# Second chunk pair's backward inverses moved from tile to tile by the sync engine

## The chip, the cores and the metric

The kernel runs on one core of one Trainium2 chip. The metric is the device time of one execution in microseconds (us). The engines are called by the names of the profile: PE is TensorE, DVE is VectorE, ACT is ScalarE, POOL is GpSimd and SP is the sync engine, which here only waits on semaphores and issues transfers.

## What is computed

One layer of a hybrid encoder on 1024 tokens of width 1024, in float32. The part that matters here is group A, a bidirectional RWKV-7 time mixing with 8 heads of 64, whose recurrence per token and direction is

```python
Sa = einsum('zbhij,zbhj->zbhi', S, at)
S  = S * wt[..., None, :] + Sa[..., :, None] * bt[..., None, :] + vt[..., :, None] * kt[..., None, :]
y  = einsum('zbhij,zbhj->zbhi', S, rt)
```

Group B is a windowed attention (128 keys to each side, distance penalty, a sink logit). Both group outputs go through one output projection and a residual, then a gated feed-forward with a width-3 convolution, and a last RMSNorm.

## The kernel before

The recurrence is done in chunks of 32 tokens (`C = 32`, `NC = 32` chunks). Within a chunk the delta rule is a triangular system, so for each chunk and head a 32x32 inverse is built beforehand. `TI[z]` holds those inverses for direction z (0 forward, 1 backward), with 4 head pairs times 32 chunks on the 128 partitions and the 32x32 matrix of one head of the pair along the free axis (`e` is the head of the pair). VectorE fills `TI[0]` and then `TI[1]` by forward substitution, two operations per row (lines 1969 and 1973), and counts rows in `sol_row`. GpSimd then stores them to DRAM as `TI_d` (line 1664 for z = 0, line 1678 for z = 1, eight transfers each, one per head pair and head), from where the scan loads them in another layout: in `TIs[slot]` the 32 rows of an inverse lie on 32 partitions.

The scan (`chunk_steps` on TensorE) takes one forward and one backward chunk per step, two steps per slot, two slots, so four steps per iteration i, and eight iterations. Slot 0 and slot 1 have each a set of tiles (`AGB`, `UV`, `TIs`, `Ys`). One step is: products with the loaded values (line 924), with the state (line 937), attention scores or probabilities in between (lines 875, 885), the product with the inverse (line 960), then state (975) and output (984). A slot's first step waits for `scan_full[slot]`, which counts all loads of that slot's tiles, 16 for each transfer. The attention scores of a slot's first step wait for `qk_full`, the loads of `q_d` and `kk_d` (line 489).

The forward inverses of the first two chunk pairs are loaded from `TI_d` early. For the backward direction the first chunks needed are the last ones, and `TI[1]` is complete only when the scan could start. So for slot 0 the kernel does not go through DRAM: SP (head 0, line 520) and ACT (head 1, line 1320) copy, for each of 2 chunks and 4 head pairs, one partition of `TI[1]` onto 32 partitions of `TIs[0]`, 4 KB each. Each of them then adds one to `moves_issued`. GpSimd waits for 2 of it, then issues the eight stores of `TI[1]`, and then waits for the first filling of slot 1 (`scan_full[1]`), after which it reloads the last five of the eight 512 KB tiles of x (`x_load`, line 1670). SP, after its eight copies, waits for all eight stores (`TI1_stored`), loads slot 1's backward inverses from `TI_d` (`load_inverses(1, 1)`, line 502, two transfers of 32 KB), and enters its loop. There it waits for step 2's products, issues `load_scan` of slot 0's next tiles (lines 474, 479, 482: ten transfers, 1.9 MB), four stores of y (532), and then `load_qk` for the next attention block (489).

`Ys[1]` lies where `TI[1]` lay, and `xT` where the first layer's operands lay, which is why ACT waits before its third output copy (line 1392) and GpSimd before `x_load`.

## Time and profile before

| | us |
|---|---|
| three runs | 1379.25, 1374.97, 1375.43 |
| their median | 1375.43 |
| the profiled execution's own time | 1381.39 |
| span of its profile | 1379.4 |
| mean granted TensorE clock | 0.962 |

The 2.0 us between the profiled time and the span lie outside the profiled instructions. Times inside the trace count from the span's start. The place of the change is the start of the scan, near 346 to 390 us of the span.

### The profile page before, as it was taken

Reading aid. Unit: us, or ns where it says so; the run is one execution under the profiler, and the core shown is the slowest. Engines: PE = TensorE matmul, PEld = TensorE weight load, DVE = VectorE, ACT = ScalarE, POOL = GpSimd, SP = SyncE. Lnnn points to the kernel's source line nnn. Section 1 sums busy time; section 2 is a strip of 40 time slices with the busy share of each in tenths; the row PEclk is TensorE's granted clock in tenths of the full one; section 3 lists DMA queues with packets and bytes.
Section 4 is the critical chain, followed back from the end, with each engine's and each line's share of the span. In section 5 each row is a group of like instructions: output and inputs, shape, how many; then the busy total and the mean of one; then the engine's idle time right before and its main releaser. Section 6 shows DMA issues by size and latency. Waiting matters only on the chain.

```text
span 1379.4 us, 28338 instructions
## 1 busy us (share of the span) xinstructions
PE 1281.8 (93%) x11280; PEld 1001.4 (73%) x11280; DVE 857.1 (62%) x1094; ACT 521.9 (38%) x729; POOL 231.2 (17%) x242
## 2 busy tenths in 40 slices
PE   6999999897589988889999999999999999999997
PEld 2476776775356655567778888888888888888886
DVE  4986687799557777783398555565555573333345
ACT  3735345221246656742144333333333342111221
POOL 1001001021312233400005222222222110000000
PEclk9999999999669989999989999999999999999998
DMA  5038758697666776502313222333222455322103
GB/s 212 20 92 188 173 149 200 182 257 181 162 203 214 237 219 208 173 31 98 131 46 92 76 68 85 91 91 87 66 76 91 137 176 208 114 97 72 49 31 123
DMA packets 145830, 179.53 MB, mean 130 GB/s; under 512 B 52432, under 2 KB 107792, under 8 KB 145776
## 3 DMA queue, kind: packets, MB, share of 16 engines
q1 hardware_dynamic: 136384, 152.16, 36.9%
q0 software_dynamic: 4288, 12.98, 3.4%
q10 hardware_dynamic: 5104, 13.67, 3.1%
q8 instruction: 34, 0.56, 0.2%
q14 instruction: 20, 0.16, 0.0%
HBM read 121.16 MB, written 57.54 MB: 130 GB/s over the span
## 4 chain that ended last, share of the span: by engine, by line
PE 75%; DVE 11%; DMA 5%; issue 3%; SPq 3%; ACT 2%; POOL 2%; DVEq 0%; ACTq 0%; POOLq 0%
PE banks L1107 28%; PE banks L695 18%; PE banks L677 6%; PE banks L1144 5%; PE banks L683 3%; DVE work L1969 2%; DVE work L1973 2%; PE banks L1081 2%; PE banks L659 2%; PE banks L885 2%; PE banks L901 1%; DMA work<-y_d 1%; DMA work<-in_w_in 1%; PE banks L1089 1%; PE banks L975 1%
## 5 line engine op out<-in xcount | busy, mean ns | idle before, releaser
L1107 PE MATMUL banks<-op,sw_hi 128*128 128x512 f32 x1120 | 344.8, 389 | 0.0
L1107 PEld LDWEIGHTS banks<-op,sw_hi 128*128 128x128 f32 x1120 | 210.3, 188 | 43.7
L1107 PE MATMUL banks<-op,sw_lo 128*128 128x512 f32 x560 | 217.8, 389 | 0.0
L2162 DVE TENSOR_TENSOR xT<-xT,banks 128x1024 f32<-128x1024 f32 x23 | 28.1, 1221 | 150.4 <-PE banks L695 150.4
L1107 PEld LDWEIGHTS banks<-op,sw_lo 128*128 128x128 f32 x560 | 105.1, 188 | 21.7
L1477 ACT ACTIVATE sw_hi<-work 128x1024 fp32r<-128x1024 f32 (+1 forms) x60 | 72.1, 1203 | 112.2 <-PE banks L1107 110.1
L1765 DVE TENSOR_TENSOR sw_lo<-work,sw_hi 128x1024 fp32r<-128x1024 f32 (+1 forms) x60 | 84.9, 1416 | 37.5 <-ACT sw_hi L1477 37.5
L677 PE MATMUL banks<-ph_hi,pw_hi 128*128 128x512 f32 x272 | 87.7, 404 | 6.4 <-DVE work L1887 3.1
L1739 POOL TENSOR_TENSOR work<-work 128x512 f32<-128x512 f32 x20 | 28.4, 1418 | 387.0 <-DMA work<-in_w_gu 245.9
L677 PE MATMUL banks<-ph_hi,pw_lo 128*128 128x512 f32 x272 | 86.2, 399 | 0.0
L695 PE MATMUL banks<-g_hi,down_hi 128*128 128x512 f32 x256 | 79.0, 390 | 0.0
L695 PE MATMUL banks<-g_hi,down_lo 128*128 128x512 f32 x256 | 78.8, 389 | 0.0
L695 PE MATMUL banks<-g_lo,down_hi 128*128 128x512 f32 x256 | 78.8, 389 | 0.0
L1407 ACT ACTIVATE down_hi<-work 128x1024 fp32r<-128x1024 f32 (+1 forms) x18 | 18.5, 1035 | 134.2 <-PE banks L695 128.8
L677 PEld LDWEIGHTS banks<-ph_hi,pw_hi 128*128 128x128 f32 x272 | 51.3, 193 | 21.6 <-issue 7.8
L683 PE MATMUL banks<-ph_lo,pw_hi 128*128 128x512 f32 x272 | 64.4, 389 | 0.0
L1689 POOL TENSOR_TENSOR work<-work 128x384 f32<-128x384 f32 x60 | 48.2, 834 | 87.1 <-DVE work L2021 87.1
L1522 ACT ACTIVATE hT<-banks,par 128x1024 f32<-128x1024 f32 x20 | 22.4, 1118 | 103.9 <-DVE banks L2252 103.9
L1644 POOL DMA_DIRECT2D work<-scan_d x32 | 20.5, 648 | 241.6 <-DMA scan_d<-work 241.3
L677 PEld LDWEIGHTS banks<-ph_hi,pw_lo 128*128 128x128 f32 x272 | 52.5, 193 | 11.4
L683 PEld LDWEIGHTS banks<-ph_lo,pw_hi 128*128 128x128 f32 x272 | 51.1, 188 | 10.6
L695 PEld LDWEIGHTS banks<-g_hi,down_hi 128*128 128x128 f32 x256 | 47.9, 188 | 10.3 <-DVE g_lo L1765 0.5
(277 smaller groups left out, 2492.4 us busy)
## 6 DMA issues: line engine op xcount, KB each, us to landing
work<-scan_d SPq DMA_DIRECT2D x32, 768.0 KB, 4.8
work<-in_w_gu SPq DMA_DIRECT2D x88, 256.0 KB, 4.6
scan_d<-work SPq DMA_DIRECT2D x16, 1024.0 KB, 5.3
g_d<-hT SPq DMA_DIRECT2D x22, 512.0 KB, 2.9
scan_d<-work SPq DMA_DIRECT2D x32, 256.0 KB, 6.6
work<-in_w_down SPq DMA_DIRECT2D x16, 512.0 KB, 3.6
work<-in_w_in ACTq DMA_DIRECT2D x15, 512.0 KB, 3.7
work<-g_d SPq DMA_DIRECT2D x15, 512.0 KB, 4.4
```

What stands on the lines that cost most here:

```text
L659: mm = pe.matmul(out[:, h * HALF:(h + 1) * HALF], wt[:, k, :], src[:, k, h * HALF:(h + 1) * HALF], start=(k == 0), stop=(k == kn - 1))
L677: pe.matmul(out[:, h * HALF:(h + 1) * HALF], w_[:, k, :], ph_hi[:, k, h * HALF:(h + 1) * HALF], start=(k == 0 and w_ is pw_hi[slot]), stop ...
L683: mm = pe.matmul(out[:, h * HALF:(h + 1) * HALF], pw_hi[slot][:, k, :], ph_lo[:, k, h * HALF:(h + 1) * HALF], start=False, stop=(k == KD - 1))
L695: mm = pe.matmul(out[:, h * HALF:(h + 1) * HALF], wp[slot][:, k, :], xp[k][:, h * HALF:(h + 1) * HALF], start=(opens and k == (ks or range ...
L885: mm = pe.transpose(banks[:, 4 + kb, (2 * e + hh) * P:(2 * e + hh + 1) * P], Pr[g][:, h, kb * P:(kb + 1) * P], ident[:, :])
L1107: mm = pe.matmul(banks[:, 3 * slot + bank, :], w[:, n, k * P:(k + 1) * P], x[n][:, k, :], start=(opens and k == 0 and p_ == 0), stop=(k == ...
L1144: mm = pe.matmul(banks[:, 6 * slot + i % 2, :], w[m][:, k, :], x[g][:, token_half[h]], start=(k == 0 and p_ == 0), stop=(k == fn - 1 and p ...
L1477: act.activation(sw_hi[:, lo_:hi_, :], wsrc[slot][:, lo_:hi_], ACT.Copy).then_inc(fs["w_hi"], 1)
L1689: p = pool.tensor_tensor(Pr[g][:, h, :], Pr[g][:, h, :], rinv[:, h:h + 1].broadcast_to([P, BAND]), ALU.mult)
L1739: pool.tensor_tensor(x[:, 1], x[:, 7], x[:, 6], ALU.add).then_inc(fs["sums"], 1)
L1765: tt(out, x, hi.bitcast(F32), ALU.subtract).then_inc(done, 1)
L2162: tt(x, x, product, ALU.add).then_inc(added[slot], 1)
```

## The change

After its eight copies for slot 0 and its increment of `moves_issued`, SP issues sixteen more copies of the same form, which fill `TIs[1]` from `TI[1]` for both heads of the pair. The two loads from `TI_d` (`load_inverses(1, 1)`) are gone. SP's wait for `TI1_stored` stays, now directly ahead of its loop, since later iterations read `TI_d`. The first filling of slot 1 counts 8 transfers plus 16 in place of 10, which is `SLOT1_FIRST`, and the waits on `scan_full[1]` on TensorE and GpSimd use it. ACT gets one more wait ahead of its third output copy, since that copy writes where `TI[1]` lies.

```diff
@@ -378,6 +378,7 @@
             return n - GROUPS[GROUP_OF[n]][0] + (8 if GROUP_OF[n] == 1 else 0)
 
 
+        SLOT1_FIRST = 8 + 4 * NPAIR
         V_STORES = 16 * 2 * (P // C)
 
 
@@ -519,8 +520,12 @@
                     at = C * j + NC - 2 + cc
                     sp.dma_start(TIs[0][x_rows(0, 1, C), 1, cc, j, :], TI[1][at:at + 1, 0]).then_inc(inverse_moved[1 - cc], 16)
             sp.sem_inc(s["moves_issued"], 1)
+            for cc in (1, 0):
+                for j in range(NPAIR):
+                    at = C * j + NC - 4 + cc
+                    for e in range(2):
+                        sp.dma_start(TIs[1][x_rows(e, 1, C), 1, cc, j, :], TI[1][at:at + 1, e]).then_inc(scan_full[1], 16)
             sp.wait_ge(s["TI1_stored"], 16 * 2 * NPAIR)
-            load_inverses(1, 1)
             y_rows = y_d.rearrange("z (c t) (e n) -> z c e t n", t=C, e=2)
 
             def store_y(i, slot):
@@ -915,7 +920,7 @@
                     if lead and q == 0:
                         pe.wait_ge(scan_full[slot], 16 * 8)
                     elif cc == 0:
-                        pe.wait_ge(scan_full[slot], 16 * 10 * i + 16 * (10 - 2 * (slot == 0)))
+                        pe.wait_ge(scan_full[slot], 16 * 10 * i + 16 * (SLOT1_FIRST if slot else 8))
                     pe.wait_ge(s["S_add"], n + FREE)
                     for j in range(NPAIR):
                         for z, c2 in enumerate(c2s):
@@ -1387,6 +1392,7 @@
                         if first == 0 and q == 2:
                             for moved in inverse_moved:
                                 act.wait_ge(moved, 16 * 2 * NPAIR)
+                            act.wait_ge(scan_full[1], 16 * SLOT1_FIRST)
                             act.wait_ge(s["TI1_stored"], 16 * 2 * NPAIR)
                         act.wait_ge(ys_stored[slot], 64 * i + FREE)
                         act.activation(y_move(slot, cc), banks[:, 2 * cc:2 * cc + 2, 0:256], ACT.Copy).then_inc(s["Y_out"], 1)
@@ -1677,7 +1683,7 @@
                 for e in range(2):
                     pool.dma_start(TI_d[1, e][:, :, j].rearrange("s c t -> c s t"), TI[1][C * j:C * (j + 1), e])\
                         .then_inc(s["TI1_stored"], 16)
-            pool.wait_ge(scan_full[1], 16 * 10)
+            pool.wait_ge(scan_full[1], 16 * SLOT1_FIRST)
             x_load(range(3, KD))
             pool.wait_ge(s["TI_stored"], 16 * 2 * NPAIR)
             pool.wait_ge(s["TI1_stored"], 16 * 2 * NPAIR)
```

SP's queue at this place, between the loads of the forward inverses and the loop (`work<-work` is a copy from `TI[1]` to `TIs`, `TI_d` the inverses in DRAM). Before:

```order
L502 DMA work<-TI_d 32x256 x3
L520 DMA work<-work 32x1x32 [waits sol_row,scan_full0,va_stored]
L520 DMA work<-work 32x1x32 x7
L502 DMA work<-TI_d 32x256 [waits TI1_stored]
L502 DMA work<-TI_d 32x256
L547 UNCONDITIONAL_BRANCH
L474 DMA work<-scan_d 128x1536 [waits S_mm,Y_mm]
L479 DMA work<-TI_d 32x256
L482 DMA work<-v_d 32x2x256
L479 DMA work<-TI_d 32x256
L482 DMA work<-v_d 32x2x256
```

With the change:

```order
L503 DMA work<-TI_d 32x256 x3
L521 DMA work<-work 32x1x32 [waits sol_row,scan_full0,va_stored]
L521 DMA work<-work 32x1x32 x7
L527 DMA work<-work 32x1x32 x16
L552 UNCONDITIONAL_BRANCH [waits TI1_stored]
L475 DMA work<-scan_d 128x1536 [waits S_mm,Y_mm]
L480 DMA work<-TI_d 32x256
L483 DMA work<-v_d 32x2x256
L480 DMA work<-TI_d 32x256
L483 DMA work<-v_d 32x2x256
```

Sixteen copies stand where two loads from `TI_d` stood, and the wait for `TI1_stored` has moved from ahead of those loads to behind the copies, onto the loop's entry; the sequence after it is the same.

GpSimd's queue at the same place. Before:

```order
L1670 DMA xT<-in_xT 128x1024 [waits qkv_mm]
L1670 DMA xT<-in_xT 128x1024 x2
L1678 DMA TI_d<-work 32x32x32 [waits moves_issued,sol_row]
L1678 DMA TI_d<-work 32x32x32 x7
L1670 DMA xT<-in_xT 128x1024 [waits scan_full1]
L1670 DMA xT<-in_xT 128x1024 x4
```

With the change:

```order
L1676 DMA xT<-in_xT 128x1024 [waits qkv_mm]
L1676 DMA xT<-in_xT 128x1024 x2
L1684 DMA TI_d<-work 32x32x32 [waits moves_issued,sol_row]
L1684 DMA TI_d<-work 32x32x32 x7
L1676 DMA xT<-in_xT 128x1024 [waits scan_full1]
L1676 DMA xT<-in_xT 128x1024 x4
```

No row moved: the stores still wait for `moves_issued`, and the five loads of x for `scan_full[1]`, whose count is now reached by copies and not by loads from `TI_d`.

## Rows read from the trace of the kernel before

**Rows 1.** The page: its first line and the shares of the chain by engine.

```profile
span 1379.4 us, 28338 instructions
...
PE 75%; DVE 11%; DMA 5%; issue 3%; SPq 3%; ACT 2%; POOL 2%; DVEq 0%; ACTq 0%; POOLq 0%
```

**Rows 2.** TensorE in order of time: start, length, row, [idle before it <-releaser].

```profile
359.34 0.65 PE L984 MATMUL banks<-work 32*32 32x64 f32 x32
366.37 1.13 PE L924 MATMUL banks<-work 32*64 32x64 f32 x32 [6.38 <-DMA work<-TI_d]
...
386.29 1.65 PE L875 MATMUL banks<-work 64*128 64x384 f32 x4 [2.38 <-DMA work<-kk_d]
```

**Rows 3.** The chain that ended last, 325 to 415 us: start, length, what.

```profile
351.46 0.02 SPq L521
...
357.57 6.63 DMA TI_d<-work
...
365.17 0.36 SPq L474
...
369.23 1.42 SPq L479
...
373.88 12.37 DMA work<-kk_d
```

**Rows 4.** GpSimd's queue in order of time, 340 to 392 us.

```profile
352.08 6.28 POOL L1678 DMA_DIRECT2D TI_d<-work  x8 [16.51 <-SPq L521]
366.62 2.68 POOL L1670 DMA_DIRECT2D xT<-in_xT  x5 [8.27 <-DMA work<-TI_d]
```

**Rows 5.** Stretches: us of each engine, PEclk, DMA share, GB/s.

```profile
core 0: us, PE busy (x) PEld busy (x) DVE busy (x) ACT busy (x) POOL busy (x), PEclk, DMA share, GB/s
360.00:362.00 2.00, 0.00 (x0) 0.00 (x0) 1.37 (x5) 1.29 (x3) 0.00 (x0) 0.72 0.87 117
362.00:364.00 2.00, 0.00 (x0) 0.00 (x0) 0.00 (x0) 0.02 (x1) 0.00 (x0) 0.50 0.07 21
364.00:366.00 2.00, 0.00 (x0) 0.00 (x0) 0.00 (x0) 0.00 (x0) 0.00 (x0) 0.50 0.10 33
366.00:368.00 2.00, 1.63 (x52) 1.51 (x56) 0.00 (x0) 0.00 (x0) 1.38 (x3) 0.50 0.83 264
...
372.00:376.00 4.00, 3.99 (x132) 2.89 (x128) 2.14 (x6) 2.00 (x6) 0.47 (x1) 0.68 1.02 400
...
384.00:388.00 4.00, 1.71 (x11) 0.64 (x15) 0.40 (x2) 0.98 (x3) 0.00 (x0) 0.50 0.97 321
```

**Rows 6.** Line 520, the first pair's moves: issue in ns, and landing.

```profile
L520 SPq DMA_DIRECT2D work<-work x8: 591/608/803, 346.0 to 350.8; - x8
...
DMA to landing us min/median/max: 1.8/1.9/2.2
```

**Rows 7.** Line 502 in 364 to 366 us, the two loads taken out.

```profile
L502 SPq DMA_DIRECT2D work<-TI_d x2: 317/368/418, 364.2 to 364.6; - x2
...
DMA to landing us min/median/max: 1.7/1.7/1.7
```

**Rows 8.** VectorE in order of time, the end of the second step.

```profile
360.31 0.69 DVE L2095 TENSOR_TENSOR work<-work,PC 128x512 f32<-128x512 f32 x1
```

**Rows 9.** DMA queues (packets, MB, share) during the moves, 346 to 352 us.

```profile
q10 hardware_dynamic: 384, 0.03, 4.7%
q1 hardware_dynamic: 336, 0.03, 4.1%
```

**Rows 10.** DMA queues during GpSimd's stores, 351 to 366 us.

```profile
q0 software_dynamic: 384, 1.05, 52.3%
```

**Rows 11.** TensorE in order of time, one stop that no row names.

```profile
409.07 0.36 PE L937 MATMUL banks<-work 64*64 64x64 f32 x1 [2.58 <-issue]
```

**Rows 12.** Line 1244 at 309 us, a load beside GpSimd's earlier stores.

```profile
L1244 ACTq DMA_DIRECT2D work<-in_w_in x1: 334/334/334, 309.4 to 309.4; - x1
...
DMA to landing us min/median/max: 3.5/3.5/3.5
```


## The prediction

> **What bounds the kernel now.** I read the page first. The span is 1379.4 us and three quarters of the chain is PE work [rows 1]; transfers hold 5% of it and SP's issuing 3%, so only a place where the chain leaves PE can give something to a change of transfers. The second view is PE in order of time around the start of the scan. Step 2 ends its output products at 359.34 + 0.65 = 359.99 us, and step 3, the first on slot 1, starts at 366.37 after 6.38 us of idleness that a load from `TI_d` ended. A second stop follows soon: the scores of iteration 1 start at 386.29 after 2.38 us of waiting for `kk_d` [rows 2].
>
> The third view is the chain between the two stops, to see what each waits on [rows 3, 4]. SP signals its moves as issued at 351.46. GpSimd starts its eight stores at 352.08, the last one's issue begins at 357.57, and all have landed 6.63 us later, at 364.20. Then SP issues the two loads of line 502, which landed before PE's 366.37 and before GpSimd starts its five loads of x at 366.62. SP enters its loop and issues the next `load_scan` from 365.17 on. Everything from there to the issue of `kk_d` at 373.88 is SP issuing without a gap, and `kk_d` takes 12.37 us to land. So PE's first stop hangs on the landing of the inverses, but the chain goes past PE: it goes over `TI1_stored`, SP's issuing and the `kk_d` transfer, and PE waits for that once more.
>
> The fourth view is the DMA share in stretches [rows 5]. It is 0.87 while the stores run (360 to 362 us), 0.07 and 0.10 in the next two stretches, 0.83 in 366 to 368, and 1.02 and 0.97 later, up to `kk_d`'s landing. The engines of the DMA are full nearly from 366 to 386 us. That is why a 384 KB load takes 12.37 us there.
>
> **The change, part by part.**
>
> *Sixteen moves more on SP.* The form is that of line 520: 8 issues of 591 to 803 ns, landing after 1.8 to 2.2 us [rows 6]. The eight issues and their gaps fill 346.02 to 351.46 us, 0.68 us each. Sixteen more from 351.48 end at 351.48 + 16 x 0.68 = 362.4; the last starts at 361.7 and lands 1.9 us later, at 363.6. I add 0.3 us for the stores beside them: 363.9. What could make this shorter is that the first eight were issued while ACT issued its own eight; the two loads taken out needed 317 and 418 ns each [rows 7]. At 0.42 + 0.04 us the last move would start at 351.48 + 15 x 0.46 = 358.4 and land near 360.4. What could make it longer is a rival below. I take 0.68 since it is the same form on the same queue.
>
> *PE's first stop.* PE could start step 3 at 361.00 at the earliest, when DVE's scaling of the state ends (360.31 + 0.69) [rows 8]. With the moves landed at 363.9 it starts there and not at 366.37: 2.5 us earlier (bounds: 366.37 - 361.0 = 5.4 us, and nothing). What waits behind it (ACT's and DVE's copies, exponentials) comes forward with it.
>
> *The two loads taken out.* The two issues of line 502 took 0.317 and 0.418 us, with a gap of 0.05 us behind each: 0.84 us of SP's time goes, out of the 0.97 us between the end of its wait (364.20) and the first load of the loop (365.17) [rows 3, 7]. Against it stands that the moves take room from the stores, and SP still waits for the stores. Eight moves of ACT and seven of SP took 4.7% + 4.1% of 6 us, so sixteen take 0.5 us of each DMA engine [rows 9]. The stores keep those engines at 52.3% of 15 us, 7.8 us, and in 352 to 362 us they are nearly full [rows 5, 10]. If all 0.5 us is added, the stores land at 364.7. SP enters its loop 0.84 - 0.5 = 0.3 us earlier; at best 0.84. The moves themselves end at 362.4, before 364.2, so SP's extra issuing (11 us) is hidden under a wait it had anyway. That cover is 1.8 us thick.
>
> *GpSimd.* Its stores are issued as before. Its wait for slot 1's tiles now ends near 363.9 and the five loads of x, 2.5 MB, start 2.5 us earlier, at about 364.1, ahead of SP's `load_scan` and not 1.4 us behind it. Nobody needs x before the output projection, behind the whole scan, so their own landing is worth nothing; their traffic is what counts.
>
> *ACT.* Its added wait stands ahead of its third output copy, which follows step 3's output products; step 3 itself starts only when the same moves have landed: nothing.
>
> *PE's second stop.* The path is SP's loop entry, its issues up to `kk_d`, and the queue in front of `kk_d`. From the issue side it comes 0.3 us earlier (bounds 0 and 0.84). But the 12.37 us of landing are a backlog, and the backlog is x and SP's loads together. Its total is unchanged. It starts earlier: before, the DMA engines stood at 0.10 in 364 to 366 us and at 0.83 in 366 to 368. With x from 364.1 on and data moving about 1 us after an issue, some 0.9 us of the first stretch and the missing 0.17 of the second (0.3 us) get used, 1.2 us of work done ahead. If everything in the backlog shifts by that, `kk_d` lands 1.2 us earlier; if SP's issuing sets it, 0.3. I take 1.0 for the sum, nearer to the backlog because landing (12.37 us) outweighs issuing. PE is ready for the scores at 386.29 - 2.38 - 2.5 = 381.4 and would find `kk_d` at 385.3: it waits 3.9 us and not 2.4. So of the 2.5 us won at the first stop 1.5 are given back at the second.
>
> The sum: 1381.39 - 1.0 = 1380.4 us for an execution like the profiled one, which lies 6 us above the median shown; on the median it is 1375.43 - 1.0 = **1374.4 us**. Everything behind 386 us shifts as a block. What I can't price there are stops like the one of 2.58 us at 409 us for which the profile names nothing [rows 11]; I give them 1 us either way.
>
> **The rivals.**
>
> *A, the forecast:* a small gain, 0.2 to 2.5 us. Chance 0.62.
>
> *B, nothing arrives:* x's head start puts 2.5 MB ahead of SP's loads, and SP's share of the queues falls at the beginning. The row for it: SP's issue at 369.23 took 1.42 us, just after GpSimd had issued the last of the x loads [rows 3, 4], so an issue can be held up by the backlog. If that comes earlier too, the 0.3 us of issuing is eaten and `kk_d` lands when it did: 1375.4 us. Against it stands that x is done before `kk_d` in both orders. Chance 0.14.
>
> *C, slower:* the moves are slowed by the stores that they now run beside. The price per move decides. SP reached its loop at 364.20 + 0.84 = 365.04, and reaches it later than that if the sixteen take more than (365.04 - 351.48) / 16 = 0.85 us each. The nearest slow rows are 0.803, the slowest of line 520 [rows 6], and 1.42 [rows 3]. Worked out from the traffic: the stores are 384 packets in 7.8 us of 16 engines, 0.33 us each [rows 10]; ACT's eight moves are 384 packets, so 3 per engine and move [rows 9]. If each of them stands behind one packet of the stores, a move takes 3 x 0.33 = 1.0 us. Issued at that pace the sixteen end at 351.48 + 16.6 = 368.1, slot 1 is ready near 370, SP's loop starts 3 us late and the time is about 1378.4. At 1.42 us each it would be 351.48 + 23.4 = 374.9, ten microseconds late, 1385. Over 0.3% slower, 4.1 us, needs 1.1 us per move. Against it: a 512 KB load and its issue beside the earlier stores of the same form took 0.334 and 3.5 us [rows 12], no more than elsewhere, and the stores have only 24 packets per engine, so the last moves find empty queues even if the first ones wait. Chance 0.14, half of it over 0.3%. The Trainium skill ("DMA: Bandwidth & Descriptors", Queues, rings and completion order) has this as a rule: each DMA engine goes round the queues that have work and takes a whole packet from each. By that rule the moves pay a packet of the stores for each of their own, at least until the stores are through; if SP's issuing isn't held by it, the last move lands about when it would have.
>
> *D, a larger gain:* the moves are issued at 0.46 us and land at about 361, PE starts 5.4 us earlier, x's traffic falls beside the stores and into the gap, and `kk_d` comes 3 us or more earlier: 1372 us. Chance 0.10, a third of it over 0.3%.
>
> **How the numbers follow.** Within 0.3% (4.1 us, about what a measurement of this kernel can tell from no change; the three runs shown lie 4.3 us apart) are A, B, half of C and most of D. Over 0.3% faster: the rest of D, and a shift of what lies behind, 0.10. Slower: half of C and the same shift, 0.10. Same 0.80. The range: A alone gives 1372.9 to 1375.2. With C's nearer price (1378.4) on one side and D's on the other it is 1371.6 to 1378.4.
>
> **What the profile of the changed kernel would show.** Right: sixteen issues of the copy form on SP from 351.5 to about 362.4; step 3 of the scan at 363.9; `load_scan` at 364.9; x's loads from 364.1; PE's second stop, again on `kk_d`, longer than before at about 3.9 us, and iteration 1's scores near 385.3. The wrong steps would show thus: issues over 0.85 us are C; under 0.5 are D; `kk_d` landing at or behind 386.3 is B, with the stop grown to 4.9 us. The prediction fails if a later wait than `kk_d` sets iteration 1, or if stores land much later than 364.7.

## The result, and the profile after

| | before | with the change |
|---|---|---|
| median of 20 runs | 1377.72 us (1373.66 to 1383.33) | 1382.32 us (1378.01 to 1387.88) |
| ratio, 95% interval | | 1.0035 [1.0024, 1.0047] |
| the profiled execution's own time | 1381.39 | 1383.78 |
| its span | 1379.4 | 1381.7 |

The change makes the kernel slower by 0.35%, which is 4.8 us (3.3 to 6.5). The forecast was 1.0 us faster. A later measurement with six runs of the change gave 1.0056 [1.0035, 1.0076].

The last row of the inverses ends at 345.93 us in the first profile of before and at 347.48 in that of after. That is ahead of everything the change touches, so I count all times below from it and write them with a plus. The page of after, its first line and the shares of the chain by engine, beside [rows 1]:

```profile
span 1381.7 us, 28353 instructions
...
PE 74%; DVE 12%; DMA 5%; SPq 4%; issue 3%; ACT 2%; POOL 1%; DVEq 0%; ACTq 0%; POOLq 0%
```

SP's issuing grew from 3% to 4%. The chain that ended last, of after (start, length, what), at the place of [rows 3]:

```profile
352.99 0.02 SPq L522
...
354.30 0.60 SPq L527
...
354.94 1.47 SPq L527
...
356.45 1.25 SPq L527
...
357.74 1.67 SPq L527
...
362.78 1.63 SPq L527
...
364.45 0.69 SPq L527
...
368.34 0.59 SPq L527
...
369.12 0.44 SPq L475
...
377.91 11.45 DMA work<-kk_d
```

The first three of the sixteen moves take 0.56 to 0.60 us. The fourth to the ninth take 1.25 to 1.71 us each, until 364.41, the tenth 0.69, and from the eleventh on they take 0.59 again. The sixteen end at 368.94, 15.9 us after they began and not 10.9, and SP reaches its loop at +21.6 (before: 365.17 - 345.93 = +19.2). `kk_d` is issued at +30.4 and lands after 11.45 us, much like before. The moves as a group (issue in ns, landing in us), answering to [rows 6]:

```profile
L527 SPq DMA_DIRECT2D work<-work x16: 564/594/1706, 353.1 to 368.3; - x16
...
DMA to landing us min/median/max: 1.8/2.7/6.2
```

TensorE in order of time, answering to [rows 2]:

```profile
361.68 1.07 PE L989 MATMUL banks<-work 32*32 32x64 f32 x32
370.19 1.13 PE L929 MATMUL banks<-work 32*64 32x64 f32 x32 [7.43 <-DMA work<-work]
...
389.40 1.65 PE L880 MATMUL banks<-work 64*128 64x384 f32 x4 [2.36 <-DMA work<-kk_d]
```

Step 3 starts at 370.19, +22.7, after 7.43 us of idleness. Before it was +20.4 after 6.38 us. What ends the wait is now a copy from tile to tile. The scores of iteration 1 start at +41.9 (before +40.4), again after a stop for `kk_d`, of 2.36 us. GpSimd's queue, answering to [rows 4], shows the stores unchanged and the loads of x behind the last move, at +23.0 and not +20.7:

```profile
353.60 6.26 POOL L1684 DMA_DIRECT2D TI_d<-work  x8 [15.18 <-SPq L522]
370.44 2.67 POOL L1676 DMA_DIRECT2D xT<-in_xT  x5 [10.58 <-DMA work<-work]
```

The stretches (us of each engine, PEclk, DMA share, GB/s) show when the hold ends, answering to [rows 5]:

```profile
362.00:364.00 2.00, 0.76 (x30) 0.52 (x20) 1.59 (x5) 1.06 (x2) 0.00 (x0) 0.50 0.79 113
364.00:366.00 2.00, 0.00 (x0) 0.00 (x0) 0.00 (x0) 0.24 (x2) 0.00 (x0) 0.50 0.13 22
366.00:368.00 2.00, 0.00 (x0) 0.00 (x0) 0.00 (x0) 0.00 (x0) 0.00 (x0) 0.50 0.05 6
368.00:370.00 2.00, 0.00 (x0) 0.00 (x0) 0.00 (x0) 0.00 (x0) 0.00 (x0) 0.50 0.05 6
370.00:372.00 2.00, 1.81 (x60) 1.70 (x64) 0.00 (x0) 0.00 (x0) 1.56 (x3) 0.50 0.86 258
```

The DMA share is still 0.79 in 362 to 364 us and 0.13 behind it; the held issues end at the same point. Behind it the DMA engines stand at 0.05 to 0.13 for six microseconds, and nobody but SP has anything to do: it issues the last seven moves, 0.65 us each with their gaps.

Single executions of this kernel differ by some 10 us, so I took two more profiles of each kernel. The tables below use one coordinate for all: time from the last row's end to (a) the start of step 3, (b) SP's first load in its loop, (c) iteration 1's scores (first product of 64x384 that follows `kk_d`). Each is a row's start minus the end of the last row.

| profile | (a) step 3 | (b) loop | (c) scores |
|---|---|---|---|
| before | 20.4 | 19.2 | 40.4 |
| before_2 | 20.8 | 19.6 | 39.5 |
| before_3 | 19.6 | 18.4 | 38.4 |
| mean | 20.3 | 19.1 | 39.4 |
| after | 22.7 | 21.6 | 41.9 |
| after_2 | 22.6 | 21.5 | 41.8 |
| after_3 | 22.7 | 21.7 | 42.0 |
| mean | 22.7 | 21.6 | 41.9 |

The three profiles of after agree to 0.3 us, and the means lie 2.4 to 2.6 us behind before on the three marks.

### The profile page after: what moved, and what is told of

It is laid out like the page before. It is cut to its first block, busy times and chain, and to the rows that moved or that the text cites. A ratio compares the mean times of both kernels' runs of the same rounds, so it can differ in the third digit from the quotient of the medians.

```text
span 1381.7 us, 28353 instructions
## 1 busy us (share of the span) xinstructions
PE 1280.2 (93%) x11280; PEld 999.8 (72%) x11280; DVE 857.0 (62%) x1094; ACT 521.6 (38%) x729; POOL 230.3 (17%) x242
## 4 chain that ended last, share of the span: by engine, by line
PE 74%; DVE 12%; DMA 5%; SPq 4%; issue 3%; ACT 2%; POOL 1%; DVEq 0%; ACTq 0%; POOLq 0%
PE banks L1112 28%; PE banks L700 18%; PE banks L682 6%; PE banks L1149 5%; PE banks L688 3%; DVE work L1975 2%; DVE work L1979 2%; PE banks L1086 2%; DMA work<-in_w_in 2%; PE banks L664 2%; PE banks L890 1%; PE banks L906 1%; PE banks L980 1%; SPq L527 1%; PE banks L1094 1%
## 5 line engine op out<-in xcount | busy, mean ns | idle before, releaser
L1650 POOL DMA_DIRECT2D work<-scan_d x32 | 20.4, 644 | 242.9 <-DMA scan_d<-work 242.7
L688 PEld LDWEIGHTS banks<-ph_lo,pw_hi 128*128 128x128 f32 x272 | 51.1, 188 | 10.6
L700 PEld LDWEIGHTS banks<-g_lo,down_hi 128*128 128x128 f32 x256 | 48.0, 188 | 10.1
```

What stands on the lines that cost most here:

```text
L688: mm = pe.matmul(out[:, h * HALF:(h + 1) * HALF], pw_hi[slot][:, k, :], ph_lo[:, k, h * HALF:(h + 1) * HALF], start=False, stop=(k == KD - 1))
L700: mm = pe.matmul(out[:, h * HALF:(h + 1) * HALF], wp[slot][:, k, :], xp[k][:, h * HALF:(h + 1) * HALF], start=(opens and k == (ks or range ...
```

## The experiments

**Second and third profiles of both kernels.** No edit.

> The kernel before, a second profile, nothing changed. The theory so far (the stores hold back SP's moves, and that sets the loss) expects here what the first profile showed, counted from the last row of the inverses: eight moves in 5.4 us, step 3 of the scan 20.4 us after that row, the loop's first load 19.2 us after it, iteration 1's scores 40.3 us after it, each within 0.5 us. The rival (the loss lies elsewhere, since the two profiles differ by only 1.6 us at those scores while the medians differ by 4.6 us) expects a part of the trace away from this place in which this profile is shorter than the first by 2 to 4 us.

> The changed kernel, a second profile, nothing changed. Theory: again some six of the sixteen moves take 1.2 to 1.7 us to issue, all while the stores run, the others 0.59 to 0.61 us; the sixteen take 15 to 17 us; step 3 starts 22 to 23.5 us after the last row; iteration 1's scores 41.5 to 43.5 us after it. Rival: the held issues differ a lot from one execution to the next (none, or all sixteen), or the loss is found behind 400 us.

> A third profile of the kernel before, to tell the change's shift from what differs between executions: step 3 at 20.4 to 20.8 us after the last row, iteration 1's scores at 39 to 40.5 us, and TensorE at half clock for 27 to 41 us of the stretch from 15 to 90 us after the row. If the rest of the loss (beyond 2 us) lies in the clock, this profile should again stay below the two of the change (42.6 and 48.7 us).

> The changed kernel once more, timed again. Theory: 1.002 to 1.005 of before; six or seven moves held; step 3 at 22.5 to 23 us after the last row, iteration 1's scores at 41.5 to 42.5 us; half clock for more than 41 us of the stretch from 15 to 90 us after the row. If that last number falls into the range of the kernel before (27 to 41 us), the clock does not carry the rest of the loss.

Measured: the table above; six, seven and six issues were over 0.8 us in the three profiles of after. Last rows ended at 347.19 us in before_3 and 346.47 in after_3. TensorE in order of time, before_3 and then after_3:

```profile
366.82 1.13 PE L924 MATMUL banks<-work 32*64 32x64 f32 x32 [5.59 <-DMA work<-TI_d]
...
385.61 1.65 PE L875 MATMUL banks<-work 64*128 64x384 f32 x4 [0.36 <-DMA work<-kk_d]
```

```profile
369.20 1.13 PE L929 MATMUL banks<-work 32*64 32x64 f32 x32 [6.73 <-DMA work<-work]
...
388.51 1.65 PE L880 MATMUL banks<-work 64*128 64x384 f32 x4 [1.86 <-DMA work<-kk_d]
```

The hold is no accident of one execution. For the clock the third pair decides nothing. The mean granted clock from +15 to +90 us, read from one stretch each, is 0.75, 0.84 and 0.77 of full speed before, and 0.76, 0.72 and 0.77 after, and these overlap. (By the trace's clock segments the time at half clock in this stretch is 37.5, 23.9 and 34.1 us before and 35.4, 41.5 and 34.0 after. The 27 to 41, 42.6 and 48.7 us in the two expectations belong to a stretch that lies 10.5 us earlier, from +4.5 to +79.5.) The scores at the start of the second half of iteration 2 stand at +84.0, +79.9 and +82.2 before and at +85.6, +86.6 and +83.9 after: 3.3 us in the mean, with a spread of 4 us within one kernel.

**The moves away from the stores.** Two kernels: the sixteen moves ahead of the signal that starts the stores, and the same moves behind the wait for the stores.

```diff
 ahead_of_stores
-            sp.sem_inc(s["moves_issued"], 1)
             for cc in (1, 0):
...
+            sp.sem_inc(s["moves_issued"], 1)
             sp.wait_ge(s["TI1_stored"], 16 * 2 * NPAIR)
 behind_stores
             sp.sem_inc(s["moves_issued"], 1)
+            sp.wait_ge(s["TI1_stored"], 16 * 2 * NPAIR)
             for cc in (1, 0):
...
-            sp.wait_ge(s["TI1_stored"], 16 * 2 * NPAIR)
```

> The sixteen moves are issued before SP signals moves_issued, so GpSimd's stores start only behind them. Theory: with no stores in the queues every move takes 0.59 to 0.68 us to issue, the sixteen 10.3 us, and slot 1 is ready 17.8 us after the last row (20.4 before, 22.7 with the change). The stores, and with them the loop entry, come 10.3 us later than before, at 29 us after the row; the time is 4 to 8 us above before, since the traffic of x is done early and only part of the 10 us reaches kk_d. Rival (SP's moves are slow by themselves, for instance because sixteen in a row fill a queue): issues over 1 us here too, from about the fourth on.

> SP waits for the stores (TI1_stored) before it issues the sixteen moves. Theory: none is held, 0.59 to 0.68 us each; the stores land 12.2 us after they start, as before; step 3 starts 18.2 + 10.3 + 2 = 30.5 us after the last row, 10 us later than before; loop entry 28.6 us after the row, 9.4 us later than before; the time 8 to 10 us above before. Rival: issues over 1 us here too, or a time near that of the change.

The moves of ahead_of_stores and then of behind_stores as a group (issue in ns, landing in us):

```profile
L526 SPq DMA_DIRECT2D work<-work x16: 590/591/1659, 352.3 to 363.8; - x16
...
DMA to landing us min/median/max: 1.8/1.8/3.2
```

```profile
L528 SPq DMA_DIRECT2D work<-work x16: 502/590/592, 366.3 to 375.7; - x16
...
DMA to landing us min/median/max: 1.7/1.8/1.8
```

Behind the stores all of them take 0.50 to 0.59 us. Ahead of the stores fourteen take 0.59 to 0.64 and two stand alone at 1.66 and 1.43, with no store yet issued. The trace has something at both: one packet of 16 KB on a queue of the kind "instruction", from +7.44 to +8.72 and from +14.33 to +15.29, while the two issues run from +7.45 to +9.11 and from +14.22 to +15.65. The queues (packets, MB, share) in 361.0 to 362.2 us, around the second:

```profile
q1 hardware_dynamic: 96, 0.01, 6.4%
q8 instruction: 1, 0.02, 5.0%
```

No packet of that size falls on the other fourteen, or on any of the sixteen behind the stores; one of 8 KB on a second instruction queue, at +6.52, held nothing. That is a coincidence in time and not an experiment. Sixteen in a row are thus not slow by themselves: the hold of six in a row belongs to the stores. Times: 1.0061 [1.0036, 1.0087] with the loop at +29.6 and scores at +48.0; 1.0071 [1.0046, 1.0097] with the loop at +29.0 and scores at +49.2.

**Half of the cost, from either side.** In half_stores four of the eight stores are left out at this place. In eight_moves SP moves only the chunk of step 3 and loads the other as before.

```diff
 half_stores
+            for j in range(1, NPAIR, 2):
+                for e in range(2):
+                    pool.dma_start(TI_d[1, e][:, :, j].rearrange("s c t -> c s t"), TI[0][C * j:C * (j + 1), e])\
+                        .then_inc(s["TI_stored"], 16)
...
-            for j in range(NPAIR):
+            for j in range(0, NPAIR, 2):
 eight_moves
-                    at = C * j + NC - 4 + cc
+                at = C * j + NC - 3
...
             sp.wait_ge(s["TI1_stored"], 16 * 2 * NPAIR)
+            for e in range(2):
+                sp.dma_start(TIs[1][x_rows(e, 1, C), 1, 0], TI_d[1, e][:, NC - 4]).then_inc(scan_full[1], 16)
...
+                    elif lead and q == 2:
+                        pe.wait_ge(scan_full[slot], 16 * 8)
+                        pe.wait_ge(x_loaded[0], 32 + 16 * 2 * NPAIR)
+                    elif lead and q == 3:
+                        pe.wait_ge(scan_full[slot], 16 * SLOT1_FIRST)
```

> The changed kernel with half of the suspected cost: four of GpSimd's eight stores of the backward inverses are left out at this place (those of head pairs 1 and 3 are filled far earlier with the forward inverses, so later backward chunks of these pairs compute with wrong inverses). Theory (each move's packets stand behind store packets, and SP's issue is held as long as there are any): the held issues fall from 6 or 7 to 3 or 4, each still 1.2 to 1.9 us, the others stay at 0.59; the sixteen take 13 to 14 us in place of 15.8; the loop's first load comes 19 to 19.5 us after the last row, as in the kernel before; the time is within 2 us of before. Rival (the hold comes from SP issuing many moves in a row, whatever the stores do): still six or more held, 15.8 us, time as with the change, 4 to 5 us above before.

> Only the chunk that step 3 needs is moved (eight moves); the chunk of step 4 is loaded from DRAM behind the stores as before, two transfers, and TensorE waits for it at step 4. Theory: three issues at 0.6, five held at about 1.5, so the eight end 9.5 to 10.5 us after they start, 15.5 us after the last row, under SP's wait for the stores; step 3 starts 17.5 to 18.5 us after the row (20.6 before), the loop's first load 19.3 to 19.8 us after it as before; the time is that of before to within 1.5 us, since only the chain over SP and kk_d counts. Rival (TensorE's first stop counts by itself): 2 to 3 us faster than before.

The chain of half_stores at its moves, every issue over 0.7 us and those behind them:

```profile
355.96 2.26 SPq L527
...
358.27 1.27 SPq L527
...
359.58 1.25 SPq L527
...
360.88 0.59 SPq L527
...
362.78 1.68 SPq L527
...
364.50 0.59 SPq L527
```

Three in a row and one alone are held, and the sixteen take 14.2 us. The stores' packets run until the end of the three; the one alone (+14.26 to +15.94) has none beside it, but a 16 KB packet of the instruction queue (+14.35 to +15.57). The marks are +21.0, +19.9 and +40.5, and the time is 1.0008 [0.9991, 1.0024]. In eight_moves, the moves as a group and then TensorE's step 3:

```profile
L526 SPq DMA_DIRECT2D work<-work x8: 565/1512/1600, 354.9 to 363.3; - x8
...
DMA to landing us min/median/max: 2.1/4.9/6.1
```

```profile
368.56 1.13 PE L935 MATMUL banks<-work 32*64 32x64 f32 x32 [5.16 <-DMA work<-work]
```

Five are held at 1.5 to 1.6 us, but the eight end at +15.4, under SP's wait for the stores. Step 3 starts at +19.2, 1.1 us earlier than the mean before, the loop at +19.9, the scores at +40.6, and the time is 0.9999 [0.9981, 1.0016]. The hold is still there and the loss is gone: it costs where it outlasts SP's wait. The earlier step 3 brought nothing that can be seen, but it did not come alone: x (+21.3) and the loop were 0.8 us later than the mean before, and the interval is 2.4 us to each side.

**More issued early.** In early_given, on the kernel before, SP issues the six loads of the next `load_scan` that need no inverse ahead of its wait for the stores. eight_and_given has this and the eight moves.

```diff
 early_given
             sp.sem_inc(s["moves_issued"], 1)
+            sp.wait_ge(s["Y_mm"], 2)
+            sp.wait_ge(s["S_mm"], 2)
+            load_scan(1, 0, inverses=False)
             sp.wait_ge(s["TI1_stored"], 16 * 2 * NPAIR)
...
-                        load_scan(i + 1, slot)
+                        load_scan(i + 1, slot, given=last > 1 or slot == 1)
```

> The kernel before, with no extra move; SP issues the six transfers of the next load_scan that don't need the stores (state operands and values) before it waits for the stores, and only the four loads of inverses behind it. It takes 2.7 us off the chain from the stores to kk_d and puts data into the empty stretch of the queues. Theory (the chain over SP's issuing and the backlog sets iteration 1): kk_d is issued about 25 us after the last row in place of 28.5, iteration 1's scores start 36.5 to 38 us after it in place of 39.9, and the time falls by 2 to 4 us; the stores may end up to 1.5 us later. Rival (kk_d is a matter of the total traffic alone or the stores are slowed as much as is won): within 1 us of before.

> Both edits of the two kernels ahead of this one in the same call: eight moves, and the six transfers issued before the wait for the stores. Theory: the eight moves end 15.5 us after the last row, after TensorE's step 2 (14.1 us), so the six transfers start 1.4 us later than in early_given; step 3 starts at 18 us, kk_d is issued at 25.5 us, iteration 1's scores start at 37 to 38.5 us; the time 1.5 to 4 us below before, no better than early_given by more than 1 us. Rival (the first stop counts): 2 to 3 us better than early_given.

Both are slower than before: 1.0030 [1.0012, 1.0049] and 1.0026 [1.0010, 1.0043]. The chain of early_given shows what went wrong:

```profile
366.90 5.25 DMA work<-TI_d
```

The inverses' loads, two of 32 KB which landed 1.7 us after their issue before [rows 7], now take 5.25 us beside 1.8 MB. Step 3 starts at +24.8, x at +25.1, the scores at +41.6. In eight_and_given step 3 starts at +19.2 and the scores at +36.2, 3.2 us earlier than before, and yet the time isn't better. I come back to that with x_later.

**Which lateness costs.** late_entry, late_both and late_both_ten put five or ten small stores of 4 KB into SP's queue, behind or ahead of the loads of line 502. In late_traffic they stand behind, and GpSimd's x waits for them. late_step3 holds TensorE alone.

```diff
 late_entry: five, late_traffic: ten
             load_inverses(1, 1)
+            for n in range(5):
+                sp.dma_start(pad_d[n], par[0:C, 0:C]).then_inc(x_loaded[0], 16)
 late_both: five, late_both_ten: ten
+            for n in range(5):
+                sp.dma_start(pad_d[n], par[0:C, 0:C]).then_inc(x_loaded[0], 16)
             load_inverses(1, 1)
 late_traffic
             pool.wait_ge(scan_full[1], 16 * 10)
+            pool.wait_ge(x_loaded[0], 32 + 160)
 late_step3
             x_load(range(3, KD))
+            pool.sem_inc(s["zero_made"], 1)
...
+                    if lead and q == 2:
+                        pe.wait_ge(s["zero_made"], 8)
```

> The kernel before plus five small stores (4 KB each, to a place that nobody reads) that SP issues behind the loads of line 502 and ahead of its loop. They cost SP's queue about 2.2 us, while the queues of the DMA engines are empty; TensorE's step 3 and the loads of x come as before. It makes the change's delay of the loop (19.4 to 21.6 us after the last row) without its moves. Theory (the loss is the delay of the loop, about one for one): 1.5 to 3 us above before. Rival (the late start of step 3 and of the x loads counts as well, or the moves do harm in another way): within 1 us of before.

> The same five small stores, issued ahead of the loads of line 502: step 3, the loads of x and the loop all come 2.2 us later than before, as they do with the change. Theory: if these three delays are all that the change does, the time is that of the change, 3.3 to 6.5 us above before. Rival (one for one only): 1.5 to 3 us above before, the same as late_entry, and the rest of the change's 4.8 us is due to something else, such as the traffic of the moves.

> The kernel before, with TensorE's step 3 held by a semaphore until GpSimd has issued its loads of x: step 3 starts about 23.5 us after the last row in place of 20.6, while x and SP's loop come as before. Theory P (TensorE's first stop costs by itself): 2 to 5 us above before. Theory T (the start of the traffic sets kk_d, and with it iteration 1; TensorE's lateness is taken up by the stop for kk_d): within 1 us of before.

> The kernel before plus ten small stores (4 KB each, read by nobody) behind the loads of line 502, which GpSimd's loads of x wait for too: both streams of the backlog start 4 to 5 us late (x at 26, the loop at 24 us after the last row), step 3 starts on time (20.6). Theory T: 4 to 8 us above before. Theory P: within 1.5 us of before.

> Twice the dose of late_both: ten small stores ahead of the loads of line 502, so step 3, x and the loop all come 4.4 us later than before. Theories T and P both expect twice what late_both showed, 5 to 9 us above before; near 4 us (no more than late_both) would say that late_both's 4.0 us were half chance.

| kernel | (a) step 3 | x issued | (b) loop | (c) scores | ratio, 95% interval |
|---|---|---|---|---|---|
| before (mean of 3) | 20.3 | 20.5 | 19.1 | 39.4 | |
| the change (mean of 3) | 22.7 | 22.9 | 21.6 | 41.9 | 1.0035 [1.0024, 1.0047] |
| late_entry | 19.6 | 19.8 | 20.6 | 38.6 | 0.9994 [0.9980, 1.0008] |
| late_step3 | 21.7 | 19.8 | 18.2 | 39.8 | 1.0011 [0.9990, 1.0032] |
| late_both | 22.5 | 22.8 | 21.3 | 40.4 | 1.0029 [1.0009, 1.0050] |
| late_both_ten | 24.2 | 24.5 | 23.0 | 43.5 | 1.0026 [1.0006, 1.0046] |
| late_traffic | 19.4 | 25.2 | 23.7 | 43.8 | 1.0050 [1.0028, 1.0072] |

A loop that is 1.5 us late, as SP's row of late_entry shows, costs nothing that can be seen (0.8 us faster, interval 2.8 us faster to 1.1 slower), where 1.5 to 3 us were expected:

```profile
364.92 0.36 SPq L475 DMA_DIRECT2D work<-scan_d  x1
```

With all three late and no extra move (late_both), step 3 starts as late as with the change, and the loss is 4.0 us (1.2 to 6.9), the size of the change's:

```profile
370.17 1.13 PE L927 MATMUL banks<-work 32*64 32x64 f32 x32 [7.00 <-DMA work<-TI_d]
```

In late_traffic TensorE's step 3 is on time and the stop has moved to `kk_d`, and this is the largest loss of the five:

```profile
367.42 1.13 PE L927 MATMUL banks<-work 32*64 32x64 f32 x32 [3.92 <-DMA work<-TI_d]
...
391.81 1.65 PE L878 MATMUL banks<-work 64*128 64x384 f32 x4 [2.24 <-DMA work<-kk_d]
```

So the lateness of TensorE is neither needed for the loss (late_traffic) nor enough for it (late_step3, whose dose was small, 1.4 us, and whose interval reaches to 1.0032). late_both_ten is the miss here: twice the dose gave no more than late_both, where 5 to 9 us were expected. One of the two measured by chance too much or too little; both intervals hold 1.0035. In the one profile of late_both nothing is left of the lateness at the next scores (+53.0; before 53.0 in the mean), so its loss rests on the timing alone.

No run delays x with SP's loop on time, so the two streams can't be told apart. What the kernels do show together is that the loss goes with the lateness of iteration 1's scores, whichever way it was made:

| kernel | scores later than before | time over before |
|---|---|---|
| late_entry | -0.8 | -0.8 |
| late_step3 | 0.4 | 1.5 |
| late_both | 1.0 | 4.0 |
| half_stores | 1.1 | 1.1 |
| eight_moves | 1.2 | -0.1 |
| early_given | 2.2 | 4.1 |
| the change | 2.5 | 4.8 |
| late_both_ten | 4.1 | 3.6 |
| late_traffic | 4.4 | 6.9 |
| change_early_x | 4.7 | 5.8 |
| ahead_of_stores | 8.6 | 8.4 |
| behind_stores | 9.8 | 9.8 |

Both columns are in us. The scores are those of one profile each (of three for the change), and they differ by 2 us among the three of before; the times are good to 2 to 4 us. Within that the two agree one for one. The three kernels whose scores came earlier than in any profile before are not in the table; they don't follow it, as the next group shows.

**Moving x.** x_later and x_later_eight put GpSimd's loads of x behind its first normalisation, on before and on eight_moves. change_early_x lets x start with the stores' landing, in the changed kernel.

```diff
 x_later
-            x_load(range(3, KD))
...
             normalised(0, 0)
+            x_load(range(3, KD))
 change_early_x
-            pool.wait_ge(scan_full[1], 16 * SLOT1_FIRST)
+            pool.wait_ge(s["TI1_stored"], 16 * 2 * NPAIR)
             x_load(range(3, KD))
```

> The kernel before, with GpSimd's five loads of x behind its first normalisation instead of ahead of it, so that they start about 34 us after the last row and not 21 us. Theory (kk_d's 11 to 12 us are a backlog of x and of SP's loads together): kk_d lands 4 to 7 us after its issue, TensorE doesn't stop for it, iteration 1's scores start 37 to 38.5 us after the last row in place of 39.9, and the time falls by 1 to 4 us. Rival (the traffic of x is only shifted onto the loads of iteration 2): same as before within 1 us.

> The same move of the x loads on the kernel with eight moves. Theory: with kk_d out of the way the first stop counts, so that here the earlier step 3 (19.2 us after the last row against 20.6) gives another 1 to 1.5 us: 2 to 5 us below before. Rival: no better than x_later.

> The changed kernel with one wait exchanged: GpSimd's loads of x wait for the stores (TI1_stored) and not for slot 1's tiles, so they start 18.5 to 19 us after the last row in place of 22.9; SP's sixteen moves are held as before and the loop starts at 21.6 us, step 3 at 22.6 us or a little later. Theory T: with x early only SP's stream is late, as in late_entry, and the time is within 1.5 us of before. Theory P: it stays 3 to 5 us above before.

TensorE in order of time in x_later, whose last row ended at 345.18 us:

```profile
380.16 0.92 PE L875 MATMUL banks<-work 64*128 64x384 f32 x4
...
384.97 0.44 PE L937 MATMUL banks<-work 64*64 64x64 f32 x10
388.68 0.57 PE L937 MATMUL banks<-work 64*64 64x64 f32 x22 [3.27 <-issue]
```

The scores start at +35.0, 4.4 us earlier than before, with no stop for `kk_d`. But a stop of 3.27 us follows within the next step, one for which the profile names no releaser, and the time is 1.0012 [0.9995, 1.0029]; x_later_eight gives 1.0018 [1.0001, 1.0035], with stops of that kind of 1.71 and 2.68 us. eight_and_given has one of 3.87 us. Before and after have no such stop at this place. What was won is lost there: the scores of iteration 1's second half start at +53.2, +58.0 and +54.9 in the three kernels and at +55.1, +51.1 and +52.7 in the profiles of before.

The stop stands in the middle of a group of 32 products, for which the program waits only at their start, so it is no wait for data. It belongs to a place in TensorE's program: it stands behind the tenth product in x_later, and behind the ninth in the two kernels with eight moves, which put two more waits into that program ahead of it (a product is two instructions, a load of weights and a matmul). The stop near +63, which all twenty profiles have [rows 11], moves likewise from behind the 31st product to behind the 30th. And in x_later a 16 KB packet of the instruction queue starts 0.8 us into the stop; the queues (packets, MB, share) in 385 to 389 us:

```profile
q1 hardware_dynamic: 370, 0.81, 61.4%
q0 software_dynamic: 178, 0.61, 42.2%
q8 instruction: 1, 0.02, 1.7%
```

Of the 34 such stops over 0.9 us behind 340 us in all twenty profiles, 33 have a packet of this queue that starts inside them or at most 1.5 us ahead. They come every 4 to 10 us here, so one by one it could be chance; for 33 of 34 it hardly is. Both facts point to TensorE having run out of loaded code. No run was made to test that, so what ends the stop is argued and not shown. TensorE's step 3 in change_early_x:

```profile
375.77 1.13 PE L929 MATMUL banks<-work 32*64 32x64 f32 x32 [12.38 <-DMA work<-work]
```

Step 3 starts at +27.4 and not +22.7: the last moves now land under x's 2.5 MB. The scores start at +44.1, the time is 1.0042 [1.0024, 1.0060]. It was meant to take one delay away and put a larger one in its place, so it doesn't tell what x's lateness costs.

## Why the prediction was wrong

**Sixteen moves at 0.68 us, landed at 363.9: the step that failed.** Counted from the last row they were to land at +18.0; they landed near +22.6. I priced them by the first pair's moves, which ran in empty queues, and added 0.3 us for the stores. Beside the stores six or seven of them took 0.81 to 1.87 us, seventeen of the nineteen in three profiles 1.22 or more. It is rival C, to which I gave 0.14, and its mechanism was right: held only while store traffic runs (behind_stores, half_stores), then back at 0.59. Its price, three packets of the stores per move or 1.0 us, was too small by a third for a held move (1.55 us in the mean of six). Over all sixteen it came out by luck, 15.9 us or 0.99 each, since ten went out at 0.56 to 0.69. In 356.4 to 362.74 us, inside the held stretch, the queues of after (packets, MB, share) read:

```profile
q0 software_dynamic: 264, 0.73, 91.6%
q1 hardware_dynamic: 143, 0.01, 1.8%
```

Four moves were issued in it, and 264 packets of the stores went by on 16 engines, 4.1 on each per issue and not 3. At 0.33 us each [rows 10] that is 1.4 us per issue, an estimate, where 1.25 to 1.71 were seen. The Trainium skill ("DMA: Bandwidth & Descriptors", Queues, rings and completion order) says that a DMA engine goes round its queues by whole packets; that small moves are slowed by another queue's traffic agrees. Its packet is a group of about 9 to 17 descriptors, and no run shows how many of the profile's packets make one, so the one to one that I took for rival C is not its rule.

**The row against it was the wrong row.** I set rival C aside by a load issued in 0.334 us beside the earlier stores [rows 12]. It was not beside them. It was issued at 309.42, 0.2 us after GpSimd began to issue the first of those stores, and their first packet moves at 312.0. The queues in 309 to 311.4 us are one, the load's own:

```profile
q10 hardware_dynamic: 71, 0.29, 42.3%
```

With the change it is the same: the first three moves end at +7.4, the first packet of the stores moves at +7.53 to +7.75, and the fourth move, issued at +7.46 to +7.50, is the first one held, in all three profiles of after and in half_stores and eight_moves. So these three don't show that a few moves are free beside the stores. (In change_early_x the last three moves were issued beside the first packets of x, at 0.59, 0.59 and 0.72 us, so a few may be free there.) The row for the price of line 520 was the wrong one for the same reason: no store's packet moves during those eight.

**The cover of 1.8 us.** SP's extra issuing was to end 1.8 us before the stores land. It ends at 368.94, +21.5, and sets the loop by itself: +21.6 in place of +19.1. The stores landed 0.7 us later than before (359.1 + 7.3 = 366.4, +18.9, against +18.3), near my 0.5.

**The second stop.** That PE would stop for `kk_d` once more held in all three profiles, though not that the stop grows to 3.9 us (2.36, 0.63 and 1.86), since step 3 was late and not early. That the backlog and not SP's issuing alone sets `kk_d` agrees with late_entry, which with x on time lost nothing to be seen, and late_traffic, which with both streams late lost 6.9 us (3.9 to 9.9); a late x by itself was not tried. The sign then followed from the first step: slot 1's readiness releases x, the held moves also delay the loop, so both streams start 2.4 to 2.6 us late. Step 3's own start, which I priced at 2.5 us with 1.5 given back, showed no worth in eight_moves, where it came 1.1 us early. The 1.2 us that x was to do ahead in the empty queues were not there to win: before, GpSimd issues x at 366.62 and its first packet moves at 369.17, 2.5 us later and not about 1 us, so x issued at 364.1 would have moved nothing until 366.6.

**The size.** The three marks are 2.4 to 2.6 us late; the timing says 3.3 to 6.5. At the mark in iteration 2 the profiles are 3.3 us apart, which the timing's lower end allows. The rest may be the clock (0.75, 0.84 and 0.77 of full speed before, 0.76, 0.72 and 0.77 after) or the stops without a releaser, but three profiles each, 4 us wide, don't show it. It stays open.

**The range.** It ended at 1378.4, for C at 1.0 us per move: a loop 3 us late, on 1375.43. The loop came 2.5 us late, so this end met the lateness, by the luck told above. It missed the time twice: the kernel before itself came out at 1377.72 over 20 runs, so that the three shown were too few to tell its median to 2 us, and the lateness was priced at 3 us, where the timing says 3.3 to 6.5.

No version tried beats the kernel before clear of noise. eight_moves and late_entry equal it.

## What to carry to other kernels

A queue that waits is no free place for more transfers if another queue's large stores are under way: small transfers issued then hold the issuing queue, and cost two to three times their price in empty queues. Take their price from a row at which the other queue's packets really move, and look that up in the queues' own counts: here a large store's first packet moved 1.4 to 2.8 us after its issue began. Ask of every semaphore that a new transfer feeds who else it releases: here slot 1's readiness also let 2.5 MB of x start, and where x and SP's loop were late with the waiting engine on time, the loss was no smaller.

## What the runs showed of the hardware

- Moves of 4 KB from one partition to 32 took 0.59 us of SP's queue when alone; those issued while packets of 128 KB stores from GpSimd moved took 0.8 to 1.9 us, most of them 1.2 or more, until the stores' traffic ended (19 moves in the three profiles of after).
- Two loads of 32 KB landed after 1.7 us in empty queues and the last after 5.25 us beside 1.8 MB issued just ahead of them.
- Three single moves took 1.66 and 1.43 us (ahead_of_stores) and 1.68 us (half_stores) with no packet of a store moving; at each of them one 16 KB packet of the instruction queue moved.
- GpSimd's stores of 128 KB moved their first packet 1.4 us (+6.15 to +7.56, before) and 2.8 us (309.23 to 312.0) after their issue began, its loads of x 2.6 us after (+20.69 to +23.24).
- Where the scores started 3 to 4 us earlier, with no stop for `kk_d`, stops of 1.7 to 3.9 us stood on TensorE in the middle of groups of products, in three kernels out of three (x_later, x_later_eight, eight_and_given). Two more waits in TensorE's program moved the stop by one product. Of such stops anywhere, 33 of the 34 over 0.9 us in all profiles have a 16 KB packet of the instruction queue that starts in them or at most 1.5 us ahead.
